# Gate tiles and branch products of the first block moved between the heads' steps, and three operand arrays moved to other byte offsets

## The reference, cut to what matters

```python
z = rms_norm(h, norm_mix) @ w_in            # one wide product: q, k, v of three attentions, the LRU's inputs, gz
ya = diff_attention(aq, ak, av, lam, slopes)             # 4 heads, width 512
yb = rg_lru_branch(bxin, bgate, ...)                     # width 512
yc = forgetting_attention(cq, ck, cv, logf)              # 4 heads, width 512
yd = sliding_window_sink_attention(dq, dk, dv, ...)      # 8 heads, width 512
gates = sigmoid(gz + b_gate)                             # 4 x 2048 columns
mixed = sum over n of gates[n] * (branch[n] @ w_branch[n])
h = h + mixed @ w_out
```

## Time and profile before

| | us |
|---|---|
| median of 3 runs | 4687.72 |
| the three runs | 4676.45, 4687.72, 4701.37 |
| the profiled execution's own time | 4708.54 |
| its span | 4706.6 |
| PE busy, PEld busy, DVE busy, ACT busy | 4190.7, 4105.3, 2539.7, 1988.6 |
| granted TensorE clock, mean | 0.923 |

### The profile page before, as it was taken

How to read it: one execution, slowest core, us unless ns; L and a number is a source line. 1 busy time by engine, 2 the same in 40 slices (tenths; PEclk the granted TensorE clock), 3 DMA queues, 4 the chain that set the end, 5 groups by cost and what they waited for, 6 DMA issues and landing times.

```text
span 4706.6 us, 87794 instructions
## 1 busy us (share of the span) xinstructions
PE 4190.7 (89%) x35084; PEld 4105.3 (87%) x35084; DVE 2539.7 (54%) x3441; ACT 1988.6 (42%) x2736; POOL 222.4 (5%) x166
## 2 busy tenths in 40 slices
PE   7788999999999989897799878999469974999998
PEld 6688999999999989885699878999469974999998
DVE  5445555454444454425455545677874468554554
ACT  5444444355554444323344443444114432555443
POOL 0000000000000000000000000000440026000000
PEclk8899999999999999977699989999669985999999
DMA  4234555445555534421155433555115530555553
GB/s 170 91 135 147 180 185 183 170 161 196 190 193 179 187 126 160 141 92 43 41 191 199 149 111 134 174 185 186 63 63 187 187 134 18 195 189 186 191 192 134
DMA packets 98492, 710.64 MB, mean 151 GB/s; under 512 B 10944, under 2 KB 11072, under 8 KB 14496
## 3 DMA queue, kind: packets, MB, share of 16 engines
q1 hardware_dynamic: 97344, 701.55, 43.5%
q0 software_dynamic: 992, 6.82, 0.4%
HBM read 706.23 MB, written 2.10 MB: 150 GB/s over the span
## 4 chain that ended last, share of the span: by engine, by line
PE 84%; DVE 7%; issue 4%; ACT 3%; POOL 0%; DVEq 0%; POOLq 0%; ACTq 0%
PE ps L472 16%; PE ps L477 16%; PE ps L473 16%; PE ps L514 8%; PE ps L516 8%; PE ps L521 8%; DVE oh_r L1832 1%; PE ps L544 1%; PE ps L578 1%; PE ps L499 1%; PE ps L498 1%; PE ps L500 1%; PE ps L770 1%; ACT wh L944 1%; ACT pr L1016 1%
## 5 line engine op out<-in xcount | busy, mean ns | idle before, releaser
L1317 DVE TENSOR_TENSOR wl<-raw,wh 128x1024 fp32r<-128x1024 f32 x1336 | 1624.4, 1219 | 1727.0 <-ACT wh L944 1710.9
L944 ACT ACTIVATE wh<-raw 128x1024 fp32r<-128x1024 f32 x1336 | 1407.5, 1055 | 1956.3 <-PE ps L514 660.3
L472 PE MATMUL ps<-x,wh 128*128 128x256 f32 x6848 | 1654.8, 283 | 72.5 <-DVE x L1365 41.8
L473 PE MATMUL ps<-x,wh 128*128 128x256 f32 x6848 | 1641.7, 281 | 0.0
L472 PEld LDWEIGHTS ps<-x,wh 128*128 128x128 f32 x6848 | 1313.5, 192 | 82.0 <-issue 74.7
L473 PEld LDWEIGHTS ps<-x,wh 128*128 128x128 f32 x6848 | 1313.7, 192 | 0.5
L477 PE MATMUL ps<-x,wl 128*128 128x256 f32 x6848 | 934.9, 279 | 2.5 <-DVE wl L1317 2.5
L477 PEld LDWEIGHTS ps<-x,wl 128*128 128x128 f32 x6848 | 858.6, 190 | 3.0 <-DVE wl L1317 3.0
L514 PE MATMUL ps<-xkh,wh 128*128 128x256 f32 x3328 | 803.3, 282 | 24.9 <-DVE xkl L1328 24.9
L516 PE MATMUL ps<-xkl,wh 128*128 128x256 f32 x3328 | 802.0, 281 | 0.0
L514 PEld LDWEIGHTS ps<-xkh,wh 128*128 128x128 f32 x3328 | 635.0, 191 | 25.9 <-issue 25.9
(11 more groups left out here) (304 smaller groups left out, 2551.4 us busy)
## 6 DMA issues: line engine op xcount, KB each, us to landing
raw<-in_w_in SPq DMA_DIRECT2D x184, 1024.0 KB, 4.8
raw<-in_expert_u SPq DMA_DIRECT2D x128, 1024.0 KB, 4.7
raw<-in_expert_v SPq DMA_DIRECT2D x128, 1024.0 KB, 4.7
raw<-in_w_ffn_gate SPq DMA_DIRECT2D x44, 1024.0 KB, 4.7
raw<-in_w_ffn_up SPq DMA_DIRECT2D x44, 1024.0 KB, 4.7
raw<-in_w_ffn_down SPq DMA_DIRECT2D x44, 1024.0 KB, 4.7
raw<-in_w_out SPq DMA_DIRECT2D x32, 1024.0 KB, 4.8
raw<-in_w_branch SPq DMA_DIRECT2D x16, 1024.0 KB, 4.7
```

The source lines that it names most:

```text
L472: begin(mm(o, wh[:, j, c], xh[:, kc, :], start=kc == 0, stop=False), kc % 8 == 0)
L473: mm(o, wh[:, j, c], xl[:, kc, :], start=False, stop=False)
L944: f(wh[:, u % 4, 0:width], raw[:, ring, c:c + width], ACT.Copy).then_inc(*k.up("hi"))
L1317: v.tensor_tensor(wl[:, u % 4, 0:width], raw[:, ring, c:c + width], wh[:, u % 4, 0:width].bitcast(F32), ALU.subtract).then_inc(*k.up("lo"))
```

## The change

The order of work. The loop `mix` is gone. Each head of `diff` gets the four gate tiles and the one chunk of branch products of branch 1 (the LRU, ready since before the heads); each head of `fox` gets those of branch 0 (`diff`), each pair of `swa` those of branch 2 (`fox`), and those of branch 3 (`swa`) stand at the end, unrolled. A head's own softmax steps are no longer deferred behind the next head: they stand between gate tiles of the same head. The sums go into `mix1` in SBUF branch by branch. The count of weight chunks, of tile matmuls (5280 from the first head to `w_out`) and of bytes is the same; a chunk of `w_branch` is now four pieces of 2 KB in each partition where it was one of 8 KB.

The addresses. `x2` goes from 192 to 128 mod 256, `xkh`/`xkl` from 192 to 32, `y2` (with all of the arena) from 64 to 160; `wh` and `wl` stay at 0.

```diff
-    s.append(("diff", 1, [("w_in", b + h, 0, full) for h in range(4) for b in (A_V, A_Q, A_K)]))
-    s.append(("fox", 1, [("w_in", b + h, 0, full) for h in range(4) for b in (C_V, C_Q, C_K)]))
-    s.append(("swa", 1, [("w_in", b, 0, full) for b in (D_K, D_V, D_Q, D_Q + 1, D_Q + 2, D_Q + 3)]))
-    s.append(("mix", KC // 4, [x for jj in range(4) for x in
-              [("w_in", GATES + KC * n + jj, 4, full) for n in range(4)] + [("w_branch", jj, 4, full)]]))
+    def fill(n, q):
+        return [("w_in", GATES + KC * n + 4 * q + t, 0, full) for t in range(4)] + [("w_branch", (n, q), 0, full)]
+    s.append(("diff", 1, [x for h in range(4) for x in
+              [("w_in", b + h, 0, full) for b in (A_V, A_Q, A_K)] + fill(1, h)]))
+    s.append(("fox", 1, [x for h in range(4) for x in
+              [("w_in", b + h, 0, full) for b in (C_V, C_Q, C_K)] + fill(0, h)]))
+    s.append(("swa", 1, [("w_in", b, 0, full) for b in (D_K, D_V)] +
+              [x for p in range(4) for x in [("w_in", D_Q + p, 0, full)] + fill(2, p)]))
+    s.append(("mix", 1, [x for q in range(4) for x in fill(3, q)]))
...
-        place("x2", 64, 128)
+        place("x2", 128, 256)
         x2 = sb("x2", [P, KC, 2, T], F32R)
-        place("raw", 0, 128)
+        place("raw", 0, 256)
-        place("xk", 64, 128)
+        place("xk", 32, 256)
...
-        arena0 = nc.sbuf_base + (64 - nc.sbuf_base) % 128
+        arena0 = nc.sbuf_base + (160 - nc.sbuf_base) % 256
...
+        mix1 = at("mix1", 16, [P, KC, T])
+        gt1 = at("gt1", 72, [P, 8, T])
+        mtmp1 = at("mtmp1", 58, [P, T])
+        f_h = at("f_h", 81, [P, 4 * KC], F32R)
+        f_l = at("f_l", 81.25, [P, 4 * KC], F32R)
...
+                if tensor == "w_branch":
+                    n, q = first
+                    src = src[4 * q:4 * q + 4, :, 512 * n:512 * n + 512].rearrange("t p w -> p t w")
+                    sp.dma_start(raw[:, slot, :].rearrange("p (t w) -> p t w", t=4), src).then_inc(S[f"land{slot}"], 16)
+                    return
...
+            def fill_gate(j):
+                tile_T(0 if j % 2 else 1)
+            def fill_mix(n, q):
+                if q == 0:
+                    pe.wait_ge(S["y_ready"], {1: 4, 0: 8, 2: 12, 3: 16}[n])
+                parts_T([(b, Y_AT[n], 4) for b in (7, 4, 5, 3)])
+                marks["wb", n, q] = k.n["full_v3"]
...
-            def diff_finish(hh):
...
+            for h in range(4):
+                tile_T(0)
+                tile_T(1)
+                turn_V(0, 4)
+                tile_T(0)
+                fill_gate(4 * h)
+                staged(0, 1)
+                for m in range(2):
+                    qk(2 + m, qs[:, 0], ks[:, 0], 64 * m, 64 * m + 64)
+                fill_gate(4 * h + 1)
+                fill_gate(4 * h + 2)
                 pe.wait_ge(*k.next("normed"))
                 turn_probs([0])
-                staged(2)
+                fill_gate(4 * h + 3)
+                staged(2, 4)
                 reserve(6)
-                v = vs[:, hh]
+                v = vs[:, h % 2]
                 mm(ps[:, 6, 0:P], pt[:, 0, 0:P], v[:, 0, :], start=True, stop=True)
                 mm(ps[:, 6, P:T], pt[:, 0, P:T], v[:, 0, :], start=True, stop=False)
                 mm(ps[:, 6, P:T], pt[:, 0, T:T + P], v[:, 1, :], start=False,
                    stop=True).then_inc(*k.up("full_v6"))
+                fill_mix(1, h)
                 pe.wait_ge(*k.next("a_y"))
                 reserve(7)
...
-            for _ in range(16):
-                k.n["got y_ready"] += 1
-            pe.wait_ge(S["y_ready"], k.n["got y_ready"])
-            marks["mix"] = k.n["full_v7"]
-            with k.loop("mix", pe, KC // 4):
-                for jj in range(4):
-                    for n in range(4):
-                        tile_T(n)
-                    parts_T([(4 + n, 4) for n in range(4)])
+                fill_mix(2, pair)
+            for q in range(4):
+                for t in range(4):
+                    fill_gate(4 * q + t)
+                fill_mix(3, q)
+            k.n["got y_ready"] = 16
...
+            def gate(n, j, meanwhile=None):
+                b = 0 if j % 2 else 1
+                done(b, meanwhile)
+                f(gt1[:, j % 8, :], reg(b), ACT.Sigmoid, bias=p_col("b_gate", KC * n + j)).then_inc(*k.up(f"free_a{b}"))
+                if j % 4 == 3:
+                    flag("gate_ready")
...
+                done(0)
+                evac(0, ks[:, 0])
+                gate(1, 4 * h)
+                gate(1, 4 * h + 1, lambda: exps_of([0, 1]))
+                gate(1, 4 * h + 2)
+                gate(1, 4 * h + 3, lambda: probs_out([0]))
+                mixed_in(1, h, diff_scale)
...
+            def mix_in(n, q, meanwhile=None):
+                if meanwhile is not None:
+                    meanwhile()
+                half()
+                dve.wait_ge(*k.next("gate_ready"))
+                for t, b in enumerate((7, 4, 5, 3)):
+                    j = 4 * q + t
+                    o = mix1[:, j, :] if n == 1 else mtmp1[:]
+                    take(b)
+                    v.tensor_tensor(o, reg(b), gt1[:, j % 8, :], ALU.mult).then_inc(*k.up(f"free_v{b}"))
+                    own()
+                    if n != 1:
+                        step(v.tensor_tensor(mix1[:, j, :], mix1[:, j, :], mtmp1[:], ALU.add))
+                    if t == 2:
+                        half()
...
+                chunk()
                 if h:
-                    take_y(6, h + 7)
+                    take_y(7, Y_AT[0] + h - 1)
+                chunk()
+                chunk()
+                chunk(lambda: diff_scores(h))
+                chunk(diff_probs)
+                chunk()
+                chunk()
+                mix_in(1, h, lambda: diff_end(h))
```

More of the change, by code:

```diff
@@ L647, in _, with less_cum @@
[L647 to L654, removed]
+            def less_cum(o):
+                for st in range(2):
+                    m = mm(o, cumq[:, 16 + st:17 + st].to_broadcast([P, P]), triu[:, st, :],
+                           start=False, stop=st == 1)
+                return m
@@ new lines, in _ @@
+            for h in range(4):
+                tile_T(0)
+                if h == 0:
+                    small_mm(7, 4, f_h, f_l)
+                tile_T(1)
+                turn_V(0, 4)
+                if h == 0:
+                    small_turn(7, 4, "v")
+                tile_T(0)
+                if h == 0:
+                    pe.wait_ge(*k.next("lsm_c"))
+                    reserve(7)
+                    for i in range(2):
+                        for st in range(2):
+                            m = mm(ps[:, 7, 4 * i:4 * i + 4], triu[:, st, i * P:(i + 1) * P],
+                                   cumq[:, 8 + 4 * st:12 + 4 * st], start=st == 0, stop=st == 1)
+                    m.then_inc(*k.up("full_v7"))
+                fill_gate(4 * h)
+                staged(0, 1)
+                pe.wait_ge(*k.next("cum_ready"))
+                qk(2, qs[:, 0], ks[:, 0], more=less_cum)
+                fill_gate(4 * h + 1)
+                fill_gate(4 * h + 2)
@@ L1127, in _ @@
                 exps([0, 1])
-            probs_out([0, 1])
-            with k.loop("mix", act, KC // 4) as i:
-                for jj in range(4):
-                    for n in range(4):
-                        done(n)
-                        f(gt[:, 4 * (jj % 2) + n, :], ps[:, n, 0:T], ACT.Sigmoid,
-                          bias=p_dyn("b_gate", i * 4 + (KC * n + jj))).then_inc(*k.up(f"free_a{n}"))
-                    flag("gate_ready")
-                    done_v(7, i * 4 + (marks["mix"] + jj + 1))
-            residual(mixT, "out", KC)
+            for pair in range(4):
+                done(0)
+                evac(0, qs[:, 0], 64.0 ** -0.5)
+                if pair == 0:
+                    evac(4, flat(vs[:, 0]))
+                gate(2, 4 * pair)
+                gate(2, 4 * pair + 1, lambda: exps_sinks(pair))
+                gate(2, 4 * pair + 2)
+                gate(2, 4 * pair + 3, lambda: probs_out([0, 1]))
+                mixed_in(2, pair)
+            for q in range(4):
+                for t in range(4):
+                    gate(3, 4 * q + t)
+                mixed_in(3, q)
+            residual(mix1, "out", KC)
             norm(hT)
@@ L1562, in _ @@
                 own()
-            take_y(6, 15)
+            for pair in range(4):
+                chunk()
+                chunk(lambda: swa_scores(pair))
+                chunk(swa_probs)
+                chunk()
+                chunk()
+                mix_in(2, pair, lambda: take_y(6, Y_AT[3] + pair))
+            for q in range(4):
+                for t in range(4):
+                    chunk()
+                mix_in(3, q)
             flag("masks_free")
@@ L1576, in mixed @@
                         step(v.tensor_tensor(dyn(mixT, j), dyn(mixT, j), mtmp[:], ALU.add))
-            with k.loop("mix", dve, KC // 4) as i:
-                for jj in range(4):
```

(5 more changed lines are left out.)

262 lines of the change are left out of this document (126 added, 136 removed).

## The result

| | median, us | runs | lowest to highest |
|---|---|---|---|
| before | 4683.41 | 4 | 4676.45 to 4701.37 |
| after | 4753.15 | 4 | 4743.72 to 4754.94 |

The account below looks back on a forecast made before the run. PE was taken to bound the kernel, by idle time and clock in the heads and gate loop and by matmul spacing elsewhere. 4687.7 - 52 (order) - 26 (addresses) = 4610 us, range 4555 to 4700.

Parts of the forecast that it names:

- The order of work: From the first head to w_out: 35.6 us less idle time plus 17 of clock, taken as 52 us gained.
- Idle time after: PE idle from the first head to w_out: 44.7 us left, against 80.3 before.
- `qk` behind the sigmoid: Scores wait for bank 1 until ACT's split and sigmoid end: 2.8 us five times, 1.5 seven times; 24.5 us added.
- The transpose of the diff output: Diff head's end: PE waits 2.4 us four times, 9.6 us; bank 7 free at m+7.8, m being the branch products' start.
- The chain to the cumulated gates: Its 4.1 us wait now lies beside a K tile; 1 us left.
- The clock: From the first head to w_out: 25 us regained at half speed, 8 left for new waits; gain 17 us.
- Table loads: ACT gets some 24 more, 31 us, expected to be covered by the matmul stream.
- I bound them by the two spacings seen: New distances 128, 32 and 160 were priced between 113.3 and 117.7 ns: 62 us less to 79 us more.
- for the x tiles I take 128 to give that (26 us): x matmuls at distance 128 all run at 113.3 ns, 26 us less; row and branch products keep their present mix.
- The sign of being wrong that the prediction named: Wrong if expert_u's halves don't both read 113.3 ns, or if row products read above 117.7.
- the rival for it: New distances collide in every stream: all at 117.7 ns, +79 us, order gains 40, 4727 us, slower; chance 0.11.
- Rival 2: Addresses do nothing, spacings fall as before, only the order's 52 us: 4636 us, some 20 either way; chance 0.22.

Follow-up runs that it names:

- old32: Kernel before, with its order of work, but x and row operands at 32 and branch outputs at 160; 4762.13 us.
- new32: Kernel after with x at 32 instead of 128, nothing else; 4708.84 us, ratio to before 1.0008.
- order_only: Kernel after with the addresses of before (x and row operands 192, branch outputs 64); 4654.46 us, ratio to before 0.9924.
- sig32: new32 with the scores waiting for bank 0 alone, `staged(0)` for `staged(0, 1)` behind the first gate tile; 4676.41 us, ratio to before 0.9949.
- addr_only: Kernel before with the addresses of after (x 128, row operands 32, branch outputs 160); 4802.43 us, ratio to before 1.0259.
- w_moved: order_only with the weights at 64 mod 256, so that the distances are 128, 128 and 0; 4769.83 us, one run.

## Why the prediction was wrong

**The order of work was right, in its sum and nearly in every term.** Forecast 52 us; measured 53.3 between `old32` and `new32`, and 43.6 for `order_only` against before by the medians (36 by the ratio 0.9924, whose interval is 21 us either side). The chance draws between 113.3 and 117.8 at 192 blur this second figure.

- Idle time after: forecast 44.7 us, in the trace 44.2 (`order_only`: 44.5).
- `qk` behind the sigmoid: forecast 2.8 us five times and 1.5 us seven times, 24.5; in the trace 26.1. The five are 3.0 us each, and the other seven take 26.1 - 5 x 3.0 = 11.1, 1.6 each. `sig32` shows that this was pure loss: 32.4 us come back when PE does not wait for that bank, 26.1 of them the waits and the rest, mostly, the falls of the clock behind them: the clock of the stretch up to w_out is 0.97 in `new32` (715.8 us) and 0.98 in `sig32` (680.8 us), which is some 16 us less at half speed, worth 8.
- The transpose of the diff output: forecast 2.4 us four times, in the trace 2.4 four times, with the releaser as told (DVE's products behind a split). The absolute times were late by about the same half microsecond on both sides, and that the difference came out right is in part luck: the transpose stood at m+8.35, not m+7.8, and the branch products took until m+5.95, not m+5.4 (m is 144.05 us in the head shown, and the other three read the same).
- The chain to the cumulated gates: 1 us left for it, in `order_only` 0.2. The start of w_out: 7.1 kept, 6.0 found.
- The clock: forecast 17 us gained. After, the stretch is 724.4 us at 0.97, some 43 us at half speed, against 106 before. PE was busy 4.6 us longer, but x ran slower: its 94 tiles here (5280 less 768, over 48) are 4512 matmuls, each 4.8 ns slower (118.6 ns on the mean of this stretch, where before had 113.8), 22 us. 4.6 - 22 gives 17 us gained.
- Table loads: 24 more were told, and 16 more are there (35 in this stretch, 19 before); ACT is busy for 18.6 us more there.

**The step that failed is the one on the addresses: "I bound them by the two spacings seen", and out of it "for the x tiles I take 128 to give that (26 us)".** No row showed distances 128, 32 or 160, and I took the two values of distance 192 for the only values there are. There are at least seven, from 113.3 to 120.0, and 128 has 118.67 or 120.0, none of which stood in any row. The sign of being wrong that the prediction named came with it: expert_u's halves read 118.6, not 113.3. In the profiled executions the sum closes: x 20,544 matmuls from a mean of 114.61 ns to 118.67 is +83 us; row products 9,984 from 116.33 to 116.67, +3; the order, as forecast, -52; together +34 against the measured +35.4. This is no sharp test of the 52: worked out the same way, `order_only` against before leaves 40 us for the order, after against `addr_only` 45, and `new32` against `old32` 55. The medians stand further apart (69.7 us) because the profiled execution of before lay 25 us above the median of its runs, and that of after 9 us below. The runs of before spread widely (4659 to 4740 us over all of them), as they would if its streams drew anew in each execution; those of after spread by 11 us, those of `addr_only`, at the same distances, by 26. No kernel has two traces, so a new draw in each execution is a reading and not shown. By `addr_only` the term is 104 to 121 us (its median against before's on the same chip, and the ratio of 1.0259), where I had -26.

The term also had the wrong sign for a reason that the profile did show. If a distance can do no better than make the faster of two values certain, and the kernel already has it two times in three, the gain is bounded (26 us for x, 62 for all products) and the loss is not bounded by anything seen. I wrote the rival for it ("a third spacing above 117.7 would do it with fewer") and gave it 0.11, and I priced it at 117.7 only. What spoke for it was there: the branch products at 64 ran at 118.2 in the place shown, and average 117.8 over all of that trace, so of the two distances in the trace one was slow throughout. Of three new, unseen distances the fair guess from that was "as likely slow as not".

Rival 2 had the addresses do nothing, which was also what the Trainium skill's rule on two independent SBUF read ports ("TensorE: Matmul & The Clock Gate", "Step-by-step: what each phase is for") would make of it. `w_moved` against `order_only` speaks against both: same operands, same order, only the weights 64 bytes on, and x went from 113.3 to 118.7 ns.

What the runs don't settle: why a distance has two values and what a stream's draw depends on. That weight loads and the moving stream meet in SBUF is a reading that fits the distance being what counts, and the spacing being the same whether ACT and DVE write or not, but no run shows where they meet.

## What to carry to other kernels

Where PE is one long stream, length over count of a fully busy stretch is the number to look at first, and it should be compared between streams of the same shape; a difference of 4.4 ns is worth 13.5 us over the 3072 matmuls of one half of expert_u alone. An operand's new address is not bounded by the values at the old one: measure it alone before it rides on another change, since here it hid a gain of some 50 us behind a loss twice as large. And when work is put between a producer and a consumer to hide a wait, look which bank it fills: a wait for the filler's bank (`staged(0, 1)`) made twelve new waits of 26 us that one argument took away.

## What the runs showed of the hardware that was not expected

- The spacing of the fp32r matmuls of 128x256 here depends on the distance mod 256 bytes between the moving operand and the weights in SBUF: 113.3 ns at 192 at best, 120.0 at 0 and 96, 5.9% more. At 2.4 GHz these are 272 and 288 cycles for 256 columns.
- A stream keeps its draw for thousands of matmuls (the 3072 of one half of expert_u at 117.8 and those of the other at 113.3, in before), through all four of the weights' half buffers.
- The clock and the length of a wait, in the stretch of the heads of the four traces with these waits (after, `order_only`, `new32`, `sig32`): each of the 15 waits of `qk` of 3.0 us goes with a fall of the clock that begins within 1.2 us of the wait's end and lasts 3.4 to 6.8 us; of the 16 waits of 2.4 us (the transpose), 10 do; of the 21 waits of `qk` of 1.5 to 1.6 us, none. In after, one of 3.0 and one of 1.6 us, each with the 3 us that follow it (stretches of 3.2 and 3.4 us that begin just before the wait's end; the clock is the third number from the end):

```profile
178.50:181.70 3.20, 2.88 (x12) 2.15 (x13) 0.79 (x2) 0.18 (x1) 0.00 (x0) 0.53 0.00 0
411.00:414.40 3.40, 3.22 (x17) 2.94 (x18) 0.35 (x1) 0.08 (x1) 0.00 (x0) 1.00 0.00 0
```
